# Scores of six of eight mLSTM heads as two single-pass products over stacked high and low parts

## What is computed

```
s   = einsum('bhtd,bhsd->bhts', qc, kc) * exp(d - m_t[..., None])
num = einsum('bhts,bhsv->bhtv', s, vc) + ...
den = sum(s, axis=-1) + ...
h   = num / max(|den|, exp(-m_t))
```

## Time and profile before

| | us |
|---|---|
| median of three runs | 1917.07 |
| the profiled execution's own time | 1916.13 |
| its span, first to last instruction | 1914.4 |
| the stage of the heads, from the first score product to the next stage's first instructions | 209.5 to 299.3 |
| PE busy | 1793.8 (94%) |
| VectorE busy | 1365.0 (71%) |
| ScalarE busy | 1025.9 (54%) |

### The profile page before, as it was taken

The page is one execution under the profiler, slowest core; times in us unless marked ns, Lnnn a source line. Parts: engine busy times, 40 slices in busy tenths (PEclk is TensorE's granted clock), DMA queues, the critical chain, the costliest instruction groups (busy, mean ns, idle before and its releaser), DMA issues. The chain is left out here.

```text
span 1914.4 us, 23744 instructions
## 1 busy us (share of the span) xinstructions
PE 1793.8 (94%) x8836; PEld 1476.7 (77%) x8836; DVE 1365.0 (71%) x1445; ACT 1025.9 (54%) x1237; POOL 131.3 (7%) x138
## 2 busy tenths in 40 slices
PE   7999997899999999799997769999999999999997
PEld 2687776687878877688886658888888888888886
DVE  3576357755554555677449548989889898989898
ACT  2543343532222124532344447888888887878775
POOL 2251120000000000100003020000000000000002
PEclk9899898899999999899998869999999999999999
DMA  7444601543443563344220338999999999999996
GB/s 269 174 145 143 242 1 48 172 132 132 133 135 129 166 201 127 111 165 152 93 86 1 113 144 320 354 404 356 401 356 403 354 405 352 402 351 407 350 407 226
DMA packets 147368, 433.87 MB, mean 227 GB/s; under 512 B 8106, under 2 KB 30802, under 8 KB 147165
## 3 DMA queue, kind: packets, MB, share of 16 engines
q1 hardware_dynamic: 144792, 428.56, 60.8%
q0 software_dynamic: 1152, 4.19, 0.6%
q10 hardware_dynamic: 1350, 0.11, 0.1%
HBM read 416.59 MB, written 16.25 MB: 226 GB/s over the span
## 5 line engine op out<-in xcount | busy, mean ns | idle before, releaser
L2816 DVE TENSOR_TENSOR w_low<-e_ring,w_high 128x1536 fp32r<-128x1536 f32 x383 | 611.6, 1621 | 85.5 <-ACT w_high L2720 84.6
L2720 ACT ACTIVATE w_high<-e_ring 128x1536 fp32r<-128x1536 f32 (+1 forms) x381 | 520.0, 1380 | 158.5 <-PE ps L2638 126.3
L2636 PE MATMUL ps<-w_high,list_h 128*128 128x512 f32 (+1 forms) x768 | 290.9, 379 | 4.6 <-DVE list_l L2834 4.2
L2638 PE MATMUL ps<-w_high,list_l 128*128 128x512 f32 (+1 forms) x768 | 287.1, 374 | 0.0
L2637 PE MATMUL ps<-w_low,list_h 128*128 128x512 f32 (+1 forms) x768 | 286.9, 374 | 0.0
L1705 ACT ACTIVATE fw_high<-ring 128x1024 fp32r<-128x1024 f32 x62 | 65.7, 1060 | 261.5 <-PE ps L1634 189.5
L1756 DVE TENSOR_TENSOR fw_low<-ring,fw_high 128x1024 fp32r<-128x1024 f32 x62 | 76.0, 1225 | 149.3 <-ACT fw_high L1705 149.3
L2636 PEld LDWEIGHTS ps<-w_high,list_h 128*128 128x128 f32 x768 | 144.9, 189 | 26.8 <-issue 4.6
L2638 PEld LDWEIGHTS ps<-w_high,list_l 128*128 128x128 f32 x768 | 144.6, 188 | 21.1
L2637 PEld LDWEIGHTS ps<-w_low,list_h 128*128 128x128 f32 x768 | 144.9, 189 | 20.6
L1632 PE MATMUL ps<-u_high,fw_high 128*128 128x512 f32 x352 | 140.7, 400 | 7.9 <-DVE fw_low L1756 7.9
(11 more groups left out here) (434 smaller groups left out, 3334.6 us busy)
## 6 DMA issues: line engine op xcount, KB each, us to landing
e_ring<-in_e_w_gu_dram SPq DMA_DIRECT2D x96, 1536.0 KB, 9.0
e_ring<-in_e_w_down_dram SPq DMA_DIRECT2D x48, 1536.0 KB, 9.0
bg_area<-in_mod_w_dram SPq DMA_DIRECT2D x72, 512.0 KB, 4.0
e_ring<-in_e_w_gu_dram SPq DMA_DIRECT2D x32, 1024.0 KB, 7.9
ring<-in_f_w_gu_dram SPq DMA_DIRECT2D x22, 1024.0 KB, 7.8
ring<-in_h_w_in_dram SPq DMA_DIRECT2D x10, 2048.0 KB, 8.0
e_ring<-in_e_w_down_dram SPq DMA_DIRECT2D x16, 1024.0 KB, 7.3
ring<-in_m_w_in_dram SPq DMA_DIRECT2D x6, 2048.0 KB, 9.6
```

The costliest lines, as they stand in the source:

```text
L2636: nc.tensor.matmul(out, high[:, f, :], w_high[:, c, :], start=(f == 0), stop=False)
L2638: last = nc.tensor.matmul(out, low[:, f, :], w_high[:, c, :], start=False, stop=(f == total - 1))
L2720: nc.scalar.activation(piece(k.w_high, p), raw_piece(k, p), ACT.Copy).then_inc(S.high_done, 1)
L2816: nc.vector.tensor_tensor(piece(k.w_low, p), raw_piece(k, p), piece(k.w_high, p).bitcast(F32), ALU.subtract).then_inc(S.low_done, 1)
```

## The change

For heads 2 to 7 (pairs 1, 2 and 3) the queries and keys are split into a part rounded to fp32r (high) and the rest (low). For each head three stacks of 128 rows and 512 columns are made: `k` holds the high part of the keys on the head's own 64 partitions and the low part on the other 64; `q_high` holds the high part of the queries on both halves; `q_low` their low part on both halves. A score tile is then two single-pass fp32r products over 128 rows, with the stack of keys as weights and `q_high` and `q_low` as moving data, added up in PSUM. Heads 0 and 1 keep the float32 products.

The high parts are made on ScalarE (`high`: two copies of 64 x 512 for the queries after the exponentials of turns 0, 4 and 8, and two for the keys after those of turns 1, 5 and 9). The low parts are made on VectorE (`low`: two subtractions for the queries after finish(n-1) in turns 1, 5 and 9, and two for the keys in turns 2, 6 and 10). The other half of each stack is filled by DMAs on SyncE's queue, from SBUF to SBUF: six for each pair, each of 64 rows of 2 KB, issued behind the zero fill. The product of an even head waits for all six of its pair. There are two sets of stacks, and one buffer `k_low` for the low keys. The core of the diff:

```diff
@@ SyncE, after the zero fill is issued
+            for pair in range(1, PAIRS):
+                sp.wait_ge(split_q, 2 * pair)
+                for odd in range(2):
+                    stack = words(pair, "q_high", odd)
+                    sp.dma_start(stack[other_rows[odd], :], stack[own_rows[odd], :]).then_inc(twice_in[pair % 2], 16)
+                sp.wait_ge(low_q, 2 * pair)
+                for odd in range(2):
+                    stack = words(pair, "q_low", odd)
+                    sp.dma_start(stack[other_rows[odd], :], stack[own_rows[odd], :]).then_inc(twice_in[pair % 2], 16)
+                sp.wait_ge(low_k, 2 * pair)
+                for odd in range(2):
+                    sp.dma_start(words(pair, "k", odd)[other_rows[odd], :], k.k_low.bitcast(F32)[own_rows[odd], :]).then_inc(twice_in[pair % 2], 16)
             sp.wait_ge(lists_zeroed, 16)
@@ TensorE
+            def stacked_scores(h):
+                pe.wait_ge(probs, 8 * h)
+                pair, odd = h // 2, h % 2
+                if not odd:
+                    pe.wait_ge(twice_in[pair % 2], 96 * ((pair + 1) // 2))
+                keys = stacks(pair, "k", odd)
+                for j in range(NT):
+                    bank, col = score_cols(j)
+                    t0 = 0 if j < 2 else 256
+                    out = k.ps[:, bank, col + t0:col + T]
+                    for m, kind in enumerate(("q_high", "q_low")):
+                        last = nc.tensor.matmul(out, keys[:, j * P:(j + 1) * P], stacks(pair, kind, odd)[:, t0:T],
+                                                start=(m == 0), stop=(m == 1))
+                last.then_inc(scored, 1)
             def scores(h):
+                if h >= 2:
+                    return stacked_scores(h)
@@ ScalarE, in the loop over turns, behind the exponentials of turn n
+                if n // 4 + 1 < PAIRS and n % 4 < 2:
+                    high(n // 4 + 1, "qk"[n % 4])
@@ ScalarE, high(pair, what)
+                if pair == 3 and what == "q":
+                    act.wait_ge(scored, 4)
+                if pair >= 2 and what == "k":
+                    act.wait_ge(twice_in[(pair - 1) % 2], 96 * (pair // 2))
+                for odd in range(2):
+                    rows = own_rows[odd]
+                    if what == "q":
+                        nc.scalar.activation(stacks(pair, "q_high", odd)[rows, :], k.qk[rows, pair, :], ACT.Copy).then_inc(split_q, 1)
+                    else:
+                        nc.scalar.activation(stacks(pair, "k", odd)[rows, :], k.qk[rows, 4 + pair, :], ACT.Copy).then_inc(split_k, 1)
@@ VectorE, in the loop over turns, behind weigh(n) and finish(n - 1)
+                if n // 4 + 1 < PAIRS and n % 4 in (1, 2):
+                    low(n // 4 + 1, "qk"[n % 4 - 1])
@@ VectorE, low(pair, what)
+                for odd in range(2):
+                    rows = own_rows[odd]
+                    if what == "q":
+                        dve.wait_ge(split_q, 2 * (pair - 1) + odd + 1)
+                        nc.vector.tensor_tensor(stacks(pair, "q_low", odd)[rows, :], k.qk[rows, pair, :],
+                                                words(pair, "q_high", odd)[rows, :], ALU.subtract).then_inc(low_q, 1)
+                    else:
+                        dve.wait_ge(split_k, 2 * (pair - 1) + odd + 1)
+                        nc.vector.tensor_tensor(k.k_low[rows, :], k.qk[rows, 4 + pair, :],
+                                                words(pair, "k", odd)[rows, :], ALU.subtract).then_inc(low_k, 1)
```

More of the change, by code:

```diff
@@ L1153, in score_cols @@
         return (j, 0) if j < 2 else (2, (j - 2) * 256 - 256)
+    split_q, split_k, low_q, low_k = k.sem("a_split_q"), k.sem("a_split_k"), k.sem("a_low_q"), k.sem("a_low_k")
+    twice_in = [k.sem(f"a_twice_in{n}") for n in range(2)]
+    PAIRS = HEADS // 2
+    own_rows, other_rows = (slice(0, M_DK), slice(M_DK, P)), (slice(M_DK, P), slice(0, M_DK))
+    stacks = lambda pair, kind, odd: k.stacks[(pair - 1) % 2][kind][odd]
+    words = lambda pair, kind, odd: stacks(pair, kind, odd).bitcast(F32)
     zeros_made, lists_zeroed = k.sem("a_zeros_made"), k.sem("a_lists_zeroed")
@@ L1227, in squares_of, with high @@
                                          accum_out=k.head_sum[:, i * HEADS + h:i * HEADS + h + 1]).then_inc(squares, 1)
+            def high(pair, what):
+                if pair == 3 and what == "q":
[8 more added lines that the diff above has]
+                        nc.scalar.activation(stacks(pair, "k", odd)[rows, :], k.qk[rows, 4 + pair, :], ACT.Copy).then_inc(split_k, 1)
             nc.scalar.activation(k.m_pick[0:16, :], k.ident[0:16, 0:16], ACT.Copy).then_inc(m_split, 1)
@@ L1282, in finish, with low @@
                                         den.unsqueeze(2).to_broadcast([P, NT, DV]), ALU.mult).then_inc(summed, 1)
+            def low(pair, what):
+                for odd in range(2):
[8 more added lines that the diff above has]
+                                                words(pair, "k", odd)[rows, :], ALU.subtract).then_inc(low_k, 1)
             for n in range(turns):
@@ L3059, in hybrid_mlstm_hgrn2_moe @@
         k.m_parts_high, k.m_parts_low, k.h_high, k.h_low = m_parts[:2], m_parts[2:], h_parts[:2], h_parts[2:]
+        gate_spare, ex_spare, low_spare = (resid_at - base + 2 * words) // 4 + 3 * D, ex_first + 3 * D, KD * T + 4 * T + 64 + D
+        stack_at = ({"q_high": (bg_at, bg_at + HALF), "q_low": (bg_at + D, bg_at + D + HALF), "k": (bg_at + 2 * D, bg_at + 2 * D + HALF)},
+                    {"q_high": (gate_spare, gate_spare + HALF), "q_low": (ex_spare, ex_spare + HALF), "k": (bg_at + 3 * D + HALF, low_spare)})
+        k.stacks = [{kind: [at(f"stack{n}_{kind}{odd}", HALF, first, F32R) for odd, first in enumerate(firsts)]
+                     for kind, firsts in stack_at[n].items()} for n in range(2)]
+        k.k_low = at("k_low", HALF, bg_at + 3 * D, F32R)
         area = {}
```

## The result

The changed kernel takes 1923.3 us (median of 8 runs, 1919.24 to 1928.31), the kernel before in the same comparison 1916.87 (8 runs, 1914.21 to 1921.8). The ratio is 1.0037 with a 95% interval of 1.0025 to 1.0049: slower by 0.37%. The forecast was 1920.7 us, slower in the likeliest case. That lies inside the outer range of 1914.5 to 1925.5 and just outside the 1918.5 to 1923 that the prediction gave its main case. The profiled execution has a span of 1923.5 us, 9.1 more than before. That compares one execution of each kernel. The changed kernel's, of 1925.26 us, is the second longest of its 8, which is one reason why 9.1 is more than the medians' 6.4.

A forecast was written before the change was run, and what follows sets the result against it. The heads' stage was taken as bound by a chain of waits through PE, ScalarE and VectorE. Product savings against pair 1's wait, low clock, copies, subtractions and late keys summed to +4.0 us: forecast 1920.7 us, range 1914.5 to 1925.5.

The forecast's parts named there:

- main case: Whole kernel: 1920.7 us, with a range of its own of 1918.5 to 1923 and a chance of 0.50.
- Pair 1 behind the zero fill: Head 2's start: pair 1's transfers wait for the fill on the same queue, so scores start at 238.7, before at 230.49.
- Low clock in head 2: Head 2: PE's clock is low after idling some 8 us, costing 1.6 us, with 0 and 3.2 as ends.
- Products: Stacked heads' scores on PE: 1.40 us against 2.77, saving 1.37 us per head, 8.2 us for six.
- Low keys on VectorE: Heads 1, 3 and 5: the keys' pair of subtractions between finish and weigh costs 1.20 us each.
- low queries: VectorE: the queries' pair of subtractions costs 0.5 us in heads 3 and 5, and is free in turn 1.
- Copies on ScalarE: Heads 2 and 4: the queries' copies cost 1.08 less 0.46 of slack, 0.62 us; the keys' copies are free.
- Key transfers of pairs 2 and 3: Heads 3 and 5: late low keys land after VectorE would release the next scores, 0.5 us each, ends 0 and 1.5.
- Head 4 at full clock: Head 4: full clock and 8.76 us; if the low clock stays, 1.6 us more.
- The sum: All terms: scores(7) start 5.4 us late at 286.6, head 7 gives 1.37 back, total +4.0 us.
- about 10.3 us: Heads 3 and 5: length of each, given as a sign that the prediction is right.
- (c): Pair 1's copies run at half the fill's rate, clock low through head 2: +7.8, 1924.7 us; chance 0.14.

The follow-up runs named there:

- e1: Changed kernel with the zero fill issued on ScalarE's DMA queue instead of SyncE's; ratio 1.0041 to the kernel before, stage 98.41 us.
- e7: Changed kernel with all copies and subtractions moved into existing waits, zero fill whole on SyncE's queue; ratio 1.0001 to the kernel before, stage 89.91 us.
- e8: Changed kernel with copies and subtractions moved into existing waits, zero fill whole on ScalarE's queue; ratio 0.9981 to the kernel before, stage 85.20 us.
- e10: Changed kernel plus eight float32 products keeping PE busy ahead of the wait for pair 1; ratio 1.0019 to the kernel before, stage 96.10 us.
- e4: Changed kernel with only pair 1's stacks made, read by heads 2 to 7, fill in three pieces; ratio 0.9980 to the kernel before, stage 82.95 us.
- e3: Changed kernel with stacks made and transferred but unread, all heads on float32 products; ratio 1.0075 to the kernel before, stage 99.00 us.
- e6: Changed kernel with copies and subtractions moved into existing waits, fill in three pieces; 1911.2 us against 1915.4 for the kernel before, ratio 0.9972.
- e5: Changed kernel with only pairs 2 and 3 stacked, heads 0 to 3 on float32 products, fill whole; ratio 1.0016 to the kernel before, stage 92.96 us.
- e2: Changed kernel with the zero fill in three pieces, later ones behind the transfers of pairs 1 and 2; median 1919.1 us, ratio 1.0005 to the kernel before.

## Why the prediction was right, and where its sizes were off

- **Pair 1 behind the zero fill: right, start 238.96 against 238.7.** Of its reasons one half was missing. The prediction gave the place in the queue alone; e1, e7 and e8 show that the engines' load is a second bar. The Trainium skill (DMA: Bandwidth & Descriptors, Issuing engines are not separate DMA queues) says that both queues use the same 16 engines, and e1's landings of over 7 us agree.
- **Low clock in head 2: right in kind, half the size.** Taken at 1.6 us, measured 2.9 to 3.3 (e10), the upper end of the 0 to 3.2 that it was given. The two heads of before from which 1.6 came had only their value products at the low clock; here the scores, the spread and the value products all were.
- **Products: 1.37 us a head predicted, 1.2 measured (e4).** The eight products take 1.60 us to the spread, not 1.40: the second starts 0.34 us after the first, not 0.23, and 0.21 lies ahead of the spread.
- **Low keys on VectorE: 1.20 predicted in heads 1, 3 and 5, 1.35 to 1.43 with the low queries measured (e3).** Two subtractions take 1.42 us up to the start of the next weigh, 253.98 to 255.40, not 1.20. With the stacked products the low queries cost too: head 3 is 11.22 us, of which 8.3 a plain head and 1.1 the wait; 1.8 remain, where the prediction had 0.5 + 1.2.
- **Copies on ScalarE: 0.62 predicted, 0.83 measured** (head 4: 9.13 against 8.3, and 10.34 against 9.51 in e3). Two copies of 64 x 512 delay ScalarE's next instruction by 1.31 us in head 4 (266.55 to 267.86), not 1.08; less the slack of 0.46 that is 0.85.
- **Key transfers of pairs 2 and 3: 0.5 predicted, 1.1 measured.** VectorE released scores(4) at about 261.5, and they started at 262.58. The transfer of 128 KB lands in 2.2 to 2.5 us rather than 2.0, and two issues take 1.10 us rather than 0.78 (row at 259.63 of SyncE's timeline). The 2.3 us that the prediction worked out beside its own from the Trainium skill (DMA: Bandwidth & Descriptors, Anatomy of one DMA) was the better number, though the section is on transfers that GpSimd issues and these are SyncE's.
- **Head 4 at full clock: as predicted** in the changed kernel, and in e6 and e4, but not in e5, so this isn't sure in each execution.

The sum was +4.0 us where the stage showed +8.9 in one execution and the medians 6.4. The missing 4.8: 0.3 at the start of head 2, 2.0 in head 2 (copies 0.2, products 0.2, and with head 4 as the measure 1.7 for the clock), 0.9 each in heads 3 and 5, 0.4 in head 4, and 0.2 each in heads 6 and 7 (rounded up). All terms were too favourable: the low clock by half its size, heads 3 and 5 by 0.9 us each, which lies outside the sign "about 10.3 us", the others by little. The profiled execution's +8.9 is more than double the +4.0, and the medians' 6.4 is nearer to it; how long the stage was in the executions behind the medians isn't known. So the place and the mechanism were right, the sizes weren't, and that the time came out as near as 2.6 us is in part luck. None of the rivals happened as a whole; (c) came nearest in its time, but its slow copies didn't occur: the transfers landed as forecast, and only its clock part did.

What stays open is what makes the clock fall at a given head. It fell in e2 after a pause of 2.80 us and in e5's head 4 after 2.70, not in e4 after 2.79, and not in the changed kernel's heads 4 and 6 after 2.23 and 2.24. It fell in e3's head 6 behind 1.64 us, and in heads 2 and 4 of the kernel before in unbroken work. e6 kept it at 1.00 in all stacked heads in the one execution profiled; that isn't shown for others. The medians differ by less than the stages (e6: 4.2 us against 9.0). The profiles show where some of that may lie. e6's execution was 7.2 us shorter than before's: its stage began 3.8 us sooner and was 9.0 shorter, and 5.6 were lost again later. What follows the stage took 1620.6 us in e6's and 1615.1 in before's, though no kernel here changes it; between 600 and 700 us behind the stage the clock was 0.93 in the one and 0.98 in the other. Over all twelve profiles what follows took between 1612.9 and 1620.6 us. Whether it tends to be longer behind a shorter stage isn't shown with one profile of each.

## What to carry to other kernels

A faster product on the critical path is worth its gain only where its new inputs are made inside waits that exist already: the same copies, subtractions and transfers cost 5.9 us where the changed kernel puts them (e3), and some 0.4 us over heads 2 to 6 inside waits for another engine (e6 against e4, 42.04 against 41.60). Before adding a small transfer, look at what large transfer runs then, even one that nobody waits for. Another queue alone gained 0.5 us here and early issue alone nothing. Both together took PE's wait for the transfer from 8.94 to 4.31 us (e8), cutting the large transfer in pieces to 2.80 (e2), and pieces with early issue left none (e6).

## What the runs showed of the hardware beyond that

VectorE's subtraction of 64 x 512 in SBUF, 0.68 us in the changed kernel (673 to 690 ns, six of them), took up to 1.67 us in e6, where it runs beside GpSimd's addition in SBUF. That addition took up to 1.71 us instead of 1.26. VectorE and GpSimd in e6, the two subtractions and the multiplication behind them, in heads 2 and 3:

```profile
228.10 2.42 DVE L1349 TENSOR_TENSOR stack_q_low<-big,stack_q_high 64x512 fp32r<-64x512 f32 x2
228.26 1.71 POOL L1375 TENSOR_TENSOR tok<-ex 128x512 f32<-128x512 f32 x1
230.55 0.69 DVE L1341 TENSOR_TENSOR ex<-ps,den 128x512 f32<-128x512 f32 x1
...
236.59 1.29 POOL L1375 TENSOR_TENSOR tok<-ex 128x512 f32<-128x512 f32 x1
236.74 2.39 DVE L1353 TENSOR_TENSOR k_low<-big,stack_k 64x512 fp32r<-64x512 f32 x2
```

Who starts first keeps its time. In head 2 VectorE's first subtraction (0.73 us) is ahead; the addition takes 1.71, and the second subtraction, issued while it runs, 1.66. In head 3 the addition is ahead and takes 1.29; the first subtraction takes 1.67 and the second 0.69. In heads 4 and 5 the addition takes 1.29 and 1.28 too, so there it is VectorE that loses time, not the engine that it would have waited for. Its rows in head 4 then follow each other without a gap, the second weigh starts 6.58 us after the head's first product instead of 6.43 as in head 6, and heads 3 to 5 took 8.46 to 8.49 us instead of 8.30. The Trainium skill (SBUF — State Buffer, SBUF: two separate sides) says that VectorE and GpSimd share a pair of ports under a lock, which a VectorE instruction with two inputs in SBUF takes against a GpSimd instruction that reads SBUF, and that the loser blocks until the other is done. The rows above agree with it.
